# The last block of a decoder layer's down projection, cut into two halves of its tokens

## The reference

```
def rmsnorm(x, g):
    xf = x.astype(jnp.float32)
    y = xf * lax.rsqrt(jnp.mean(xf * xf, axis=-1, keepdims=True) + EPS)
    return (y * g.astype(jnp.float32)).astype(x.dtype)
...
        # channel-mixing sub-layer: squared-ReLU MLP
        h = rmsnorm(x, norm_mlp_g[l]) * (1.0 + sc2) + sh2
        u = jnp.square(jax.nn.relu(jnp.einsum('bsd,df->bsf', h, w_up[l])))
        x = x + g2 * jnp.einsum('bsf,fd->bsd', u, w_down[l])
    return rmsnorm(x, final_g)
```

## Time and profile before

| | us |
|---|---|
| median of 3 runs | 948.97 (948.15 to 949.64) |
| profiled execution | 948.9 |
| its slowest core's span (core 4) | 947.4 |
| spans of the 8 cores | 942.5 to 947.4 |
| TensorE busy | 857.4 (91%) |
| ScalarE busy | 501.2 (53%) |
| VectorE busy | 358.9 (38%) |
| GpSimd busy | 170.5 (18%) |

### The profile page before, as it was taken

One profiled execution on the slowest core, in us unless ns is written; L12 is line 12 of the kernel. 1 busy time (PEld: TensorE's weight loads), 2 busy tenths in 40 slices (PEclk: granted clock), 3 DMA queues, 4 the chain that ended last, 5 costly groups with the idle time before them and its releaser, 6 DMA issues.

```text
span 947.4 us, 13047 instructions; the slowest of 8 cores (942.5 to 947.4 us)
## 1 busy us (share of the span) xinstructions
PE 857.4 (91%) x4421; PEld 385.7 (41%) x4421; DVE 358.9 (38%) x562; ACT 501.2 (53%) x741; POOL 170.5 (18%) x180
## 2 busy tenths in 40 slices
PE   1768879897999899999998999999999999999994
PEld 0324333433444344443443444444444444444441
DVE  1262765636453641224852122221112222111566
ACT  3055465557677878886887323234432323445543
POOL 6040212112111110245760000000000000003331
PEclk9969979989999999999999999999999999999997
DMA  8993323342311034204928005050043100000224
GB/s 183 170 173 97 101 45 56 77 95 51 57 23 23 1 89 90 90 1 167 166 54 148 1 1 89 1 90 1 15 76 55 34 1 1 1 1 1 90 89 178
DMA packets 13744, 63.50 MB, mean 67 GB/s; under 512 B 1776, under 2 KB 2032, under 8 KB 9968
## 3 DMA queue, kind: packets, MB, share of 16 engines
q0 software_dynamic: 8352, 36.41, 22.9%
q1 hardware_dynamic: 5328, 26.27, 7.9%
HBM read 90.69 MB, written 8.39 MB: 105 GB/s over the span
## 4 chain that ended last, share of the span: by engine, by line
PE 79%; ACT 7%; DVE 5%; DMA 4%; issue 4%; POOL 1%; DVEq 0%; ACTq 0%; POOLq 0%
PE ps L495 68%; PE ps L988 5%; PE ps L941 5%; DMA arena<-wada 4%; ACT arena L972 3%; DVE arena L1291 1%; PE ps L948 1%; ACT arena L1241 1%; DVE arena L550 1%; DVE arena L1024 1%; ACT arena L1004 1%; ACT arena L505 1%; ACT arena L499 1%; ACT arena L682 1%; DVE arena L1022 0%
## 5 line engine op out<-in xcount | busy, mean ns | idle before, releaser
L495 PE MATMUL ps<-arena 128*128 128x512 bf16 (+4 forms) x3685 | 765.1, 351 | 74.4 <-DMA arena<-wada 24.5
L495 PEld LDWEIGHTS ps<-arena 128*128 128x128 bf16 (+1 forms) x3685 | 322.5, 99 | 472.3 <-issue 150.5
L1273 DVE SCALAR_TENSOR_TENSOR arena<-ps,arena 128x512 f32<-128x512 f32 x128 | 95.7, 749 | 312.8 <-PE ps L495 312.8
L972 ACT ACTIVATE arena<-ps 128x1024 bf16<-128x1024 f32 x158 | 158.5, 1020 | 82.1 <-PE ps L495 44.0
L1260 ACT ACTIVATE arena<-ps 128x512 f32<-128x512 f32 x128 | 76.1, 595 | 210.0 <-PE ps L495 209.6
L641 POOL TENSOR_TENSOR arena<-arena 128x512 f32<-128x512 f32 (+2 forms) x49 | 65.2, 1331 | 183.4 <-ACT arena L1121 181.8
L941 PE MATMUL ps<-arena 128*128 128x512 bf16 (+1 forms) x320 | 87.6, 356 | 4.6 <-ACT arena L972 4.4
L1261 ACT ACTIVATE arena<-arena 128x512 bf16<-128x512 f32 x128 | 80.5, 629 | 11.9 <-ACT arena L1260 0.3
L988 PE MATMUL ps<-arena 128*128 128x512 bf16 (+1 forms) x320 | 85.6, 349 | 0.0
L980 POOL TENSOR_TENSOR arena<-arena 128x512 bf16<-128x512 f32 x32 | 41.3, 1292 | 191.5 <-ACT arena L979 171.7
L1121 ACT ACTIVATE arena<-arena 128x512 bf16<-128x512 f32 x56 | 35.3, 630 | 40.4 <-DVE arena L1273 35.8
(11 more groups left out here) (62 smaller groups left out, 337.2 us busy)
## 6 DMA issues: line engine op xcount, KB each, us to landing
arena<-wada POOLq DMA_DIRECT2D x24, 512.0 KB, 6.9
arena<-xt SPq DMA_DIRECT2D x8, 1024.0 KB, 8.9
arena<-xt SPq DMA_DIRECT2D x4, 2048.0 KB, 9.0
arena<-wup POOLq DMA_DIRECT2D x8, 1024.0 KB, 13.3
arena<-wdn POOLq DMA_DIRECT2D x8, 1024.0 KB, 18.9
out<-arena SPq DMA_DIRECT2D x12, 512.0 KB, 2.7
arena<-win POOLq DMA_DIRECT2D x11, 256.0 KB, 40.3
arena<-wo POOLq DMA_DIRECT2D x1, 2048.0 KB, 21.8
```

The lines of the kernel that those rows point to most:

```text
L495: S.op("pe", lambda h: h.matmul(bk(bank, rows, cols), lhsT=lhsT, rhs=rhs, start=start, stop=stop), r=r, w=[bankb[bank]])
L972: S.op("act", lambda h: h.activation(out=PT[p][:, :, c0:c1], in_=PS[:, b0:b0 + 2, c0:c1], func=AF.Exp, scale=sc), r=[bankb[b0], bankb[b0 + ...
L1273: S.op("dve", lambda h, b=b, fb=fb: h.scalar_tensor_tensor(out=X1T[G][:, fb, :], in0=bk(b), scalar=MODCOL[:, 40 + fb:41 + fb], in1=X1T[G][ ...
```

## The change

The last call of mlp_down, for pass 3 and group 3, is replaced by last_down. It runs the eight feature blocks twice: first for tokens 0 to 255 of the group, then for tokens 256 to 511, each with 8 matmuls of 256 columns. Folds, squares, the ones matmuls, Ln, Exp, products and stores of group 3 are all done in halves. The norm of a half is in five parts, as before: its sum, and four times two products with a store.

- The five parts of final(2), the norm of the group before, are put ahead of the blocks 1 to 5 of the first half. Before they stood ahead of the blocks 3 to 7 of the whole projection.
- In final(2) blocks 1, 3, 5 and 7 are now multiplied by the gain on ScalarE (L1284) and by RX2 on GpSimd (L1286). Before, VectorE did all eight.
- The five parts of the first half's norm are put ahead of the blocks 1 to 5 of the second half. The second half's norm comes behind its last block.
- A store of group 3 carries two feature blocks by 256 tokens (1 KB pieces) and no longer one by 512 (2 KB pieces). There are eight either way.

The core of the diff:

```
 def final(G):
-            last = G == NG - 1
+            shared = G == NG - 2
 
             def one(k):
-                if last and k % 3 == 2:
+                if shared and k % 2:
+                    S.op("act", lambda h: h.activation(out=X1T[G][:, k, :], in_=X1T[G][:, k, :], func=AF.Copy,
+                                                       scale=GCOLS[:, 2, k:k + 1]), r=[bX1[G][k], bCOLS], w=[bX1[G][k]])
                     S.op("pool", lambda h: h.tensor_tensor(out=X1T[G][:, k, :], in0=X1T[G][:, k, :], in1=RX2, op=ALU.mult),
                          r=[bX1[G][k], bRX2], w=[bX1[G][k]])
...
+        def last_down(q, G, between):
...
+            def norm(i):
+                c0, c1 = i * 256, i * 256 + 256
+
+                def total():
+                    b = rotS.next()
+                    for k in range(8):
+                        mm(b, None, (c0, c1), ONESB, SQ2[slots[k]][:, c0:c1], k == 0, k == 7, [bONES, bSQH[k][i]])
+                    S.op("act", lambda h: h.activation(out=RX2[:, c0:c1], in_=bk(b, None, (c0, c1)), func=AF.Ln, scale=1.0 / D, bias=EPSC),
+                         r=[bankb[b], bEPS], w=[bRXH[i]] + ([] if i else [bRX2]))
+                    S.op("act", lambda h: h.activation(out=RX2[:, c0:c1], in_=RX2[:, c0:c1], func=AF.Exp, scale=-0.5),
+                         r=[bRXH[i]], w=[bRXH[i]])
+
+                def one(k):
+                    if k % 3 == 2:
+                        S.op("pool", lambda h: h.tensor_tensor(out=X1T[G][:, k, c0:c1], in0=X1T[G][:, k, c0:c1], in1=RX2[:, c0:c1],
+                                                               op=ALU.mult), r=[bXH[k][i], bRXH[i]], w=[bXH[k][i]])
+                    else:
+                        S.op("dve", lambda h: h.scalar_tensor_tensor(
+                            out=X1T[G][:, k, c0:c1], in0=X1T[G][:, k, c0:c1], scalar=GCOLS[:, 2, k:k + 1], in1=RX2[:, c0:c1],
+                            op0=ALU.mult, op1=ALU.mult), r=[bXH[k][i], bCOLS, bRXH[i]], w=[bXH[k][i]])
+                    if k % 2:
+                        od = S.dma("sp", lambda h: h.dma_start(
...
+                return in_parts(total, one, 4)
+
+            def half(i, between):
+                c0, c1 = i * 256, i * 256 + 256
+                for fb in range(8):
+                    if 1 <= fb < 1 + len(between):
+                        between[fb - 1]()
+                    b = rotD.next()
+                    for fc in range(8):
+                        mm(b, None, (c0, c1), WDN[s_][:, fc, fb * 128:(fb + 1) * 128], UT[us][:, fc, c0:c1], fc == 0, fc == 7,
+                           [bWDN[s_], bUT[us][fc]])
+                    S.op("dve", lambda h, b=b, fb=fb: h.scalar_tensor_tensor(
...
+                    S.op("act", lambda h, fb=fb: h.activation(out=SQ2[slots[fb]][:, c0:c1], in_=X1T[G][:, fb, c0:c1], func=AF.Square),
...
+                    if fb % 3 == 2:
+                        S.op("act", lambda h, fb=fb: h.activation(out=X1T[G][:, fb, c0:c1], in_=X1T[G][:, fb, c0:c1], func=AF.Copy,
...
+            half(0, between)
+            between = norm(0)
+            half(1, between)
+            for f in norm(1):
+                f()
...
+            if i + 1 == len(seq):
+                last_down(q, G, final(G - 1))
+                break
             mlp_down(q, G, final(G - 1) if q == 3 and G > 0 else ())
...
-        for f in final(NG - 1):
-            f()
```

More of the change, by code:

```diff
@@ L1293, in one @@
                          r=[bX1[G][k], bCOLS, bRX2], w=[bX1[G][k]])
-                k0 = k if last else k - 1
-                if last or k % 2:
+                if k % 2:
                     od = S.dma("sp", lambda h: h.dma_start(
-                        out=out_d[G * 128:(G + 1) * 128, k0 * 512:(k + 1) * 512],
-                        in_=X1T[G][:, k0:k + 1, :].rearrange("p a b -> p (a b)")), bX1[G][k], r=bX1[G][k0:k + 1])
+                        out=out_d[G * 128:(G + 1) * 128, (k - 1) * 512:(k + 1) * 512],
+                        in_=X1T[G][:, k - 1:k + 1, :].rearrange("p a b -> p (a b)")), bX1[G][k], r=bX1[G][k - 1:k + 1])
@@ L1299, in one @@
                     S.final.append(od)
-            return in_parts(lambda: sums(G, not last), one, 4)
+            return in_parts(lambda: sums(G, True), one, 4)
+        bXH = [[Buf(f"XH{k}_{i}", bX1[NG - 1][0].alloc) for i in range(2)] for k in range(8)]
+        bRXH = [Buf(f"RXH{i}", bRX2.alloc) for i in range(2)]
+        def last_down(q, G, between):
+            s_, us = q % 2, (q * 4 + G) % 2
+            sq0 = sq2_ctr[0]
+            sq2_ctr[0] += 8
+            slots = [(sq0 + k) % NSQ2 for k in range(8)]
+            rs = [4, 5]
+            bSQH = [[Buf(f"SQH{k}_{i}", bSQ2[slots[k]].alloc) for i in range(2)] for k in range(8)]
+            def norm(i):
[16 more added lines that the diff above has]
+                            op0=ALU.mult, op1=ALU.mult), r=[bXH[k][i], bCOLS, bRXH[i]], w=[bXH[k][i]])
+                    if k % 2:
+                        od = S.dma("sp", lambda h: h.dma_start(
+                            out=out_d[G * 128:(G + 1) * 128, :].rearrange("p (k t) -> p k t", k=8)[:, k - 1:k + 1, c0:c1],
+                            in_=X1T[G][:, k - 1:k + 1, c0:c1]), bXH[k][i], r=[bXH[k - 1][i], bXH[k][i]])
+                        S.final.append(od)
+                return in_parts(total, one, 4)
[9 more added lines that the diff above has]
+                    S.op("dve", lambda h, b=b, fb=fb: h.scalar_tensor_tensor(
+                        out=X1T[G][:, fb, c0:c1], in0=bk(b, None, (c0, c1)), scalar=MODCOL[:, 40 + fb:41 + fb],
+                        in1=X1T[G][:, fb, c0:c1], op0=ALU.mult, op1=ALU.add),
+                         r=[bankb[b], bMOD[20 + fb // 2], bX1[G][fb]], w=[bXH[fb][i]] + ([] if i else [bX1[G][fb]]))
+                    S.op("act", lambda h, fb=fb: h.activation(out=SQ2[slots[fb]][:, c0:c1], in_=X1T[G][:, fb, c0:c1], func=AF.Square),
+                         r=[bXH[fb][i]], w=[bSQH[fb][i]] + ([] if i else [bSQ2[slots[fb]]]))
+                    if fb % 3 == 2:
+                        S.op("act", lambda h, fb=fb: h.activation(out=X1T[G][:, fb, c0:c1], in_=X1T[G][:, fb, c0:c1], func=AF.Copy,
+                                                                  scale=GCOLS[:, 2, fb:fb + 1]),
+                             r=[bXH[fb][i], bCOLS], w=[bXH[fb][i]])
+            half(0, between)
[3 more added lines that the diff above has]
+                f()
```

6 lines of the change are left out of this document (1 added, 5 removed).

## The result

The changed kernel takes 954.51 us (median of 4 runs, 954.36 to 956.48), and the kernel before 948.56 (947.86 to 949.64): a ratio of 1.0067, interval 1.0055 to 1.0079, so 5.2 to 7.5 us slower. The forecast was 953.8, slower.

What follows compares the result with a forecast made beforehand. TensorE was taken to set the pace until 936, then the tail of Ln, Exp, products and last store. 948.97 + 3.1 (2.9 + 2.2 + 0.9 - 2.9) + 1.7 for the clock = 953.8 us; range 951.0 to 956.0.

Steps and rivals of the forecast that it cites:

- Step 1: Group 2's sum, earlier in TensorE's queue: idle 5.1 us ahead of it, last matmul starts 2.9 us later.
- rival D: Half-width matmuls are spaced by their weight loads, 2.7 us more in all: 956.5 us; chance 0.03.
- F: Rival: group 2's sum waits less because its tree's last add comes 1.6 us sooner: 950.5 us; chance 0.04.
- Step 2: First half: ScalarE becomes the pacer, and the second half's next block waits for the half Ln: +2.2 us.
- Step 3: End of second half: the last sum matmul waits for fold and square, starting at 942.0 instead of 941.1: +0.9 us.
- Step 4: Tail in half width, last sum matmul to end of VectorE's products: 5.2 us instead of 8.07, -2.9 us.
- The sum at full clock: Whole change without any clock loss: 2.9 + 2.2 + 0.9 - 2.9 = +3.1 us, giving 952.1 us.
- Step 5: Behind the 5.1 us gap every core's TensorE falls to 1.2 GHz: +1.7 us, between 0 and 3.4.
- rival B: The clock's loss is hidden behind ScalarE's pace, or no fall comes: 952.1 us; chance 0.20.
- A second fall: Clock may fall again behind the second gap, some 2.5 us in pieces before 934.3: 0 to 1.7 us more.
- Rival C: ScalarE and VectorE keep ahead of TensorE, so only stall and shorter tail remain: 948.0 us; chance 0.05.

Runs made afterwards that it cites:

- e5_fill2: Changed kernel plus matmuls into an unread PSUM bank, 20 ahead of group 2's sum and 9 in the second gap; 952.22 us, ratio 1.0028.
- e9: e5_fill2 with all eight products of group 2's norm on VectorE, none shared with ScalarE and GpSimd; 953.91 us, ratio 1.0048.
- e6_again: The changed kernel itself, unaltered, run once more beside the others on one chip; 955.48 us, ratio 1.0065.
- e1_fill: Changed kernel plus 20 matmuls into an unread PSUM bank ahead of group 2's sum; 953.25 us, ratio 1.0051.
- e2_late: Changed kernel with group 2's norm ahead of first-half blocks 6, 7 and second-half 0 to 2, first half's norm ahead of second-half 3 to 7; 952.42 us.
- e4_pos1: Kernel before, whole width, with only group 2's norm parts moved ahead of blocks 1 to 5 instead of 3 to 7; 953.00 us, ratio 1.0037.
- e10_halves: e2_late with the first half's norm also put behind the second half's last block, so no interleaving; 949.11 us, ratio 1.0002.
- e3_noshare: Changed kernel with all eight products of group 2's norm on VectorE, without the ScalarE copies and GpSimd products; 953.27 us, ratio 1.0041.

## Why the prediction was right, step by step

**Step 1, the stall.** 5.1 us predicted, 5.13 measured, ended by the GpSimd add. The half matmuls are spaced by 0.109 at full clock, so rival D is out; and F too, since the gap is 5.12 us or more on all eight cores and not 1.6 shorter.

**Step 2, the first half.** Block 1 of the second half was to start 10.3 us behind the sum; at full clock (e5_fill2) it does at 10.6. The size was right by luck in part, since two errors in it nearly cancel. ScalarE's work from the first square behind Exp to the eighth was put at 7.2 us, and is 6.7 in e5_fill2 (924.77 to 932.46 on core 5, less its waits). Its waits for VectorE's folds were put at 0.2 us, and are 1.0:

```profile
928.62 1.36 DVE L1289 SCALAR_TENSOR_TENSOR arena<-arena 128x512 f32<-128x512 f32 x1
930.52 0.42 ACT L1363 ACTIVATE arena<-arena 128x256 bf16<-128x256 f32 x1 [0.69 <-DVE arena L1359]
```

VectorE works there without a pause from 924.82 to 931.55, with two of its four products of group 2 at 1.36 us beside GpSimd's. So ScalarE does not pace the first half alone, but in turn with VectorE; in the changed kernel it waits 2.0 us for folds on core 1 and 3.7 on core 7, and is not nearly continuous as forecast.

I also wrote that four whole copies are what makes ScalarE the later of the two, and that without them it would be done by 930.2. e9 shows that without them TensorE waits for VectorE, and 1.4 us longer. That sentence is wrong: it took work off ScalarE and did not put 4 x 0.66 us back on VectorE, which had folds to do in the same stretch.

**Step 3, the second half.** 7.7 us from block 1 to the last sum predicted, 18.25 - 10.6 = 7.7 measured. The last sum comes 18.0 us behind that of group 2 by the prediction, and 18.25 in e5_fill2.

**Step 4, the tail.** 5.2 predicted, 4.94 measured. The products take 3.49 us instead of 3.8: the two GpSimd products make two of VectorE's six last 1.04 and 0.94 us instead of 0.47, which is 1.04 us more, where 1.58 - 0.2 were forecast.

**The sum at full clock.** +3.1 predicted; 23.2 - 20.1 = +3.1 in e5_fill2. Block 1 is 0.3 later than forecast and the tail 0.3 shorter, so here too errors cancel.

**Step 5, the clock.** That every core would fall came true, and rival B is out: 1.0 us or more shows on every core. The size was taken as 1.7 for all. It is 1.0 to 1.2 on one half of the cores, where part of the slow stretch is hidden, and 2.6 to 2.85 on the other half, where the delay lets GpSimd's product come ahead of VectorE's. That order is no term of the prediction, and 1.7 lies between the two values by luck: their mean in the profiled execution is 1.95. This is the mis-sized term.

The metric is the slowest core: with one of the second kind the sum is 3.1 + 2.8 = 5.9, and the medians differ by 5.95. That they agree so well is in part chance, since the slowest core of the profiled execution (core 1) is of the first kind and is last because it reached the sum of group 2 last; in e6_again it is one of the second. So 954.5 was measured and 953.8 forecast, with a kernel before that is 0.4 faster in the runs beside it.

A second fall, behind the second gap, did not come in the changed kernel. It came in e1_fill, where the first had been prevented. What decides between the two was not tried. The sentence ahead of the prediction that only the first quarter and the last 15 us show gaps is too strong: the gaps of 2.52 us of the earlier trace rows lie near 504 and 509.

**Rival C's remark** that the stall alone eats the gain holds for the account, but not as a cause: e2_late has no such stall, and is 3.3 per mille slower than before all the same. There are two losses, each shown alone: the early sum with its fall of the clock (e4_pos1; the share of the clock in it by e5_fill2), and the first half's norm among the second half's blocks (e2_late against e10_halves). They do not add up, since TensorE waits in one place for what it did not wait for in another.

## What to carry to other kernels

A matmul that waits for a long chain belongs as far back in TensorE's queue as its result can be spared: everything behind it waits too, and the gap brings the clock down with it. Where VectorE and GpSimd take turns, a delay of 0.2 us can change which of them comes first, and here that cost more (1.45 us) than the slow clock itself (1.0 to 1.2). Before a norm is interleaved with blocks to hide it, add up what VectorE and ScalarE must do per block in the narrower width; where that is more than TensorE's time for the block, the interleaved sum stalls the blocks behind it. And look whether two engines that share out a tail really run side by side.

## What the runs showed of the hardware beyond that

- The long gaps ahead of the sum brought the clock down every time, and a shorter gap only sometimes. With the gap of 5.1 us ahead of the sum it fell on all 24 cores of the changed kernel, e6_again and e3_noshare, and with the 4.3 us of e4_pos1 on all 8. All 96 core traces of this case have a gap of 2.5 us near 505, and behind it the clock fell on 21 of them.
- The clock of a core fell behind a stretch in which TensorE was not idle but busy for 1.45 of 2.80 us (e1_fill, core 7), and did not behind the second gap of the changed kernel, in which it was busy for as little (1.51 of 2.80 us on core 2).
- The granted clock took a third level behind the sum in two runs, on two cores each: from 933.5 to 942 core 6 of e3_noshare had 0.81, as had core 2 of e5_fill2 from 936 to 941. Half matmuls came every 0.131 us there, and D1 was 1.1 to 1.3 us longer. The two late cores of e5_fill2, 0 and 1, had this level too, on and off between 25 and 186 us, and were some 5 and 10 us late at the gap near 505 already. What brings it is open.

```profile
936.00:941.00 5.00, 5.00 (x40) 4.01 (x37) 3.65 (x9) 2.84 (x8) 0.00 (x0) 0.81 0.61 210
```

- VectorE's products of two operands in on-chip memory and GpSimd's products take turns, and which starts first decides who waits; VectorE's folds, which read PSUM, do not wait. In the changed kernel six whole products of the groups 1 and 2 took 0.99 us in the mean (0.74 without GpSimd), and the folds 0.47:

```profile
L1347 DVE SCALAR_TENSOR_TENSOR arena<-ps,arena 128x256 f32<-128x256 f32 x16 | 7.3, 474 | 7.8 <-PE ps L495 7.8
L1289 DVE SCALAR_TENSOR_TENSOR arena<-arena 128x512 f32<-128x512 f32 x6 | 5.9, 990 | 0.0
```
